# Encoder layer, MLP stage: the first two output tiles made together, the last square summed by TensorE, a function table loaded at another place

## What is computed

```python
hn = modulated_rms_norm(h, sh2, sc2)            # rms_norm(h) * (1 + sc2) + sh2, over 2048 features
u = dwconv_centred(hn @ w_up[l], w_ffn_conv[l]) + b_ffn_conv[l]   # 2048 -> 2 * 5632, 3 taps over tokens
u_gate, u_val = jnp.split(u, 2, axis=-1)
h = h + gt2[:, None, :] * ((jax.nn.silu(u_gate) * u_val) @ w_down[l])
return rms_norm(h) * final_norm
```

## Time and profile before

| | |
|---|---|
| median of 3 runs | 2656.44 us (2653.32 to 2656.96) |
| profiled execution, its own time | 2658.15 us |
| its span | 2656.5 us |
| TensorE matmul busy | 2560.8 us, 96% |
| DVE busy | 1425.2 us, 54% |
| ScalarE busy | 1022.2 us, 38% |
| mean granted clock of TensorE | 0.983 of full |

### The profile page before, as it was taken

The page is one execution under the profiler, slowest core; times in us unless marked ns, Lnnn a source line. Parts: engine busy times, 40 slices in busy tenths (PEclk is TensorE's granted clock), DMA queues, the critical chain, the costliest instruction groups (busy, mean ns, idle before and its releaser), DMA issues.

```text
span 2656.5 us, 35703 instructions
## 1 busy us (share of the span) xinstructions
PE 2560.8 (96%) x12302; PEld 2098.3 (79%) x12302; DVE 1425.2 (54%) x1854; ACT 1022.2 (38%) x1428; POOL 214.3 (8%) x286
## 2 busy tenths in 40 slices
PE   4999999999999899979999999999999999999997
PEld 4777788888887688857888888888888888888885
DVE  6736666666666655464444444444444444444454
ACT  4335435434434343334443234442344432222334
POOL 3401121121121112000000000000000000000000
PEclk7999999999999999999999999999999999999998
DMA  9933454454443535323333333333333323333333
GB/s 349 317 107 111 127 154 116 133 148 120 144 140 113 151 104 155 106 63 95 95 96 91 98 103 95 95 89 98 105 95 97 100 84 98 103 95 95 89 92 127
DMA packets 431664, 318.21 MB, mean 120 GB/s; under 512 B 12886, under 2 KB 403841, under 8 KB 431105
## 3 DMA queue, kind: packets, MB, share of 16 engines
q1 hardware_dynamic: 401648, 212.19, 27.8%
q0 software_dynamic: 29184, 104.87, 12.4%
q10 hardware_dynamic: 785, 0.51, 0.1%
HBM read 313.33 MB, written 4.19 MB: 120 GB/s over the span
## 4 chain that ended last, share of the span: by engine, by line
PE 92%; DVE 3%; DMA 1%; issue 1%; ACT 1%; POOL 0%; DVEq 0%; ACTq 0%; POOLq 0%
PE pw L1399 23%; PE pw L1401 23%; PE pw L1400 23%; PE pw L1383 2%; PE pw L1384 2%; PE pw L1385 2%; PE pd L1669 2%; PE pd L1692 2%; PE pd L1705 2%; PE pd L1652 1%; PE pd L1712 1%; DMA ka<-in_w_ada_dram 1%; DMA T<-in_w_ada_dram 1%; PE pd L1728 1%; PE pd L1723 1%
## 5 line engine op out<-in xcount | busy, mean ns | idle before, releaser
L1399 PE MATMUL pw<-act_hi,w_hi 128*128 128x512 f32 x2016 | 812.7, 403 | 13.9 <-DVE act_lo L1294 8.7
L929 DVE TENSOR_TENSOR w_lo<-raw,w_hi 128x1024 fp32r<-128x1024 f32 x426 | 520.7, 1222 | 519.2 <-ACT w_hi L555 516.7
L1401 PE MATMUL pw<-act_hi,w_lo 128*128 128x512 f32 x2016 | 787.3, 391 | 0.0
L1400 PE MATMUL pw<-act_lo,w_hi 128*128 128x512 f32 x2016 | 785.6, 390 | 0.0
L555 ACT ACTIVATE w_hi<-raw 128x1024 fp32r<-128x1024 f32 x426 | 450.1, 1057 | 503.3 <-PE pw L1401 408.6
L1399 PEld LDWEIGHTS pw<-act_hi,w_hi 128*128 128x128 f32 x2016 | 379.3, 188 | 106.6 <-issue 23.8
L1401 PEld LDWEIGHTS pw<-act_hi,w_lo 128*128 128x128 f32 x2016 | 378.9, 188 | 81.4
L1400 PEld LDWEIGHTS pw<-act_lo,w_hi 128*128 128x128 f32 x2016 | 379.7, 188 | 80.3 <-issue 6.9
L1399 PE MATMUL pw<-mh_hi,w_hi 128*128 128x512 f32 x704 | 276.0, 392 | 1.6 <-DVE w_lo L929 1.6
L1401 PE MATMUL pw<-mh_hi,w_lo 128*128 128x512 f32 x704 | 274.2, 389 | 0.0
L1400 PE MATMUL pw<-mh_lo,w_hi 128*128 128x512 f32 x704 | 274.0, 389 | 0.0
(11 more groups left out here) (278 smaller groups left out, 2639.2 us busy)
## 6 DMA issues: line engine op xcount, KB each, us to landing
raw<-in_w_up_dram SPq DMA_DIRECT2D x176, 512.0 KB, 4.0
ada_w<-in_w_ada_dram POOLq DMA_DIRECT2D x128, 512.0 KB, 4.4
raw<-in_w_in_dram SPq DMA_DIRECT2D x84, 512.0 KB, 3.9
raw<-in_w_down_dram SPq DMA_DIRECT2D x64, 384.0 KB, 3.4
raw<-in_w_down_dram SPq DMA_DIRECT2D x64, 320.0 KB, 3.1
raw<-in_w_out_dram SPq DMA_DIRECT2D x32, 512.0 KB, 4.4
DD<-in_w_ada_dram POOLq DMA_DIRECT2D x9, 512.0 KB, 8.1
EG<-in_w_ada_dram POOLq DMA_DIRECT2D x9, 512.0 KB, 7.0
```

Of the source, the lines that this page charges most:

```text
L929: V.tensor_tensor(w_lo[slot][:], raw[slot][:], w_hi[slot][:].bitcast(F32), ALU.subtract).then_inc(lo_made.sem, 1)
L1399: M(bank, w_hi[slot][:, k, :], hi[:, k0 + k, :], start=first, stop=False)
L1400: M(bank, w_hi[slot][:, k, :], lo[:, k0 + k, :], start=False, stop=False)
L1401: ins = M(bank, w_lo[slot][:, k, :], hi[:, k0 + k, :], start=False, stop=last)
```

## The change

Six parts.

- SP loads the first four units of the MLP otherwise: unit MLP0+i now holds feature tiles 4i to 4i+3 of both the first gate tile and the first value tile, side by side, in two transfers of 256 KB, the second counted on a semaphore of its own (up_in).
- TensorE's `first_up` does six matmuls for each normalised tile, three for either bank. The splits of units MLP0+2 and +3 stand on ScalarE behind act_hi of tiles 6 and 10, their low halves on DVE in the passes of tiles 8 and 12. Both banks end together.
- The first tile pair's copies, convolution, Silu and product are written out ahead of the loops, which start at pass 1 in chunk 0.
- The last square before the norm isn't added by DVE. TensorE sums sqacc (15 squares) and then sq into the same bank.
- ScalarE loads the table set of Ln and Exp by name at the start of the last chunk's down stage.
- In that stage DVE multiplies by the norm's weights before it adds the square, not after.

The bodies of `convolve` and `gated` are those of the loop before, moved out of it (L1315 to L1337), and left out here.

```diff
--- before.py
+++ after.py
...
-        q_in = sem("q_in")
+        q_in, up_in = sem("q_in"), [sem(f"up_in{i}") for i in range(2)]
...
-            with sp.Fori(0, CHUNKS) as c:
-                with sp.Fori(0, FC) as f:
+            def chunk(c, first=0):
+                with sp.Fori(first, FC) as f:
                     for part in range(2):
                         tile(MLP0 + MLP_PER * c + 4 * f + 2 * part, w_up, part * DFF + (c * FC + f) * P)
                 with sp.Fori(0, KT) as m:
                     u = MLP0 + MLP_PER * c + 4 * FC + 2 * m
                     for j, (k0, n_k) in enumerate(((0, 6), (6, FC - 6))):
                         load(j, u + j, w_down[bass.ds((c * FC + k0) * P, n_k * P), bass.ds(m * P, P)], n_k)
+
+            for i in range(4):
+                sp.wait_ge(lo_made.sem, MLP0 + i - 1)
+                by_tile = raw[i % 2][:].rearrange("p (k t) n -> p k t n", t=2)
+                for t, landed in enumerate((raw_in[i % 2], up_in[i % 2])):
+                    rows_i = w_up[4 * i * P:4 * (i + 1) * P, t * DFF:t * DFF + P]
+                    sp.dma_start(by_tile[:, :, t, :], rows_i.rearrange("(k p) n -> p k n", p=P)).then_inc(landed, 16)
+            chunk(0, first=1)
+            with sp.Fori(1, CHUNKS) as c:
+                chunk(c)
...
             split((OUT0 + KT) // 2, 1)
-            with act.Fori(0, KT // 2) as i:
+            with act.Fori(0, KT // 2 - 1) as i:
                 for j in range(2):
                     split((OUT0 + KT) // 2 + i + 1, j)
                     square(2 * i + j)
+            for j in range(2):
+                act.wait_ge(up_in[j], 16)
+                split(MLP0 // 2, j)
+                square(KT - 2 + j)
 
             def inverse_rms(i):
                 act.wait_ge(*ssum.after(i))
@@ -851,11 +865,27 @@
                 act.wait_ge(*h2_step.after(0, m + 1))
                 nc.scalar.activation(act_hi[:, m, :], hn2[:, m % 2, :], ACT.Identity, bias=mod[:, 48 + m:49 + m]) \
                     .then_inc(h2_hi.sem, 1)
-
-
-            def chunk(c, last=False):
+                if m in (6, 10):
+                    act.wait_ge(up_in[(6, 10).index(m)], 32)
+                    split(MLP0 // 2 + 1, (6, 10).index(m))
+
+            def first_up(part):
+                act.wait_ge(unit_used.sem, MLP0 + 4)
+                act.wait_ge(fconv_step.sem, 3 * part + 3)
+                nc.scalar.activation(gp[:, part, 1:S + 1], pw[part][:], ACT.Copy).then_inc(up_taken.sem, 1)
+
+            split(MLP0 // 2 + 2, 0)
+            first_up(0)
+            first_up(1)
+            split(MLP0 // 2 + 2, 1)
+            act.wait_ge(fconv_step.sem, 9)
+            nc.scalar.activation(cv[:, 0, :], cv[:, 0, :], ACT.Silu).then_inc(fsilu.sem, 1)
+            act.wait_ge(*fprod.after(0))
+            nc.scalar.activation(mh_hi[:, 0, :], prod[:], ACT.Copy).then_inc(mh_hi_made.sem, 1)
+
+            def chunk(c, first=0, last=False):
                 base = MLP0 // 2 + MLP_PER // 2 * c
-                with act.Fori(0, FC) as f:
+                with act.Fori(first, FC) as f:
                     n = FC * c + f
                     pair = base + 2 * f
 
@@ -881,12 +911,13 @@
                     if last:
 
                         act.wait_ge(out_taken.sem, KT * CHUNKS + m + 1)
-                        act.wait_ge(sqacc_step.sem, KT + 1 + m)
+                        act.wait_ge(sqacc_step.sem, KT + m)
                         nc.scalar.activation(sq[:], at(hTf, m), ACT.Square).then_inc(sq_made.sem, 1)
                         if j is not None:
                             turned(m - 2, j)
 
                 if last:
+                    nc.scalar.preload_act_table_set(LOG_EXP)
                     down(0)
                     down(1)
                     with act.Fori(1, KT // 2) as i:
@@ -902,7 +933,8 @@
                 nc.scalar.activation(otok[:, :, bass.ds(m * P, P)], pd[1 + j].rearrange("p (b n) -> p b n", n=P), ACT.Copy) \
...
-            with act.Fori(0, CHUNKS - 1) as c:
+            chunk(0, first=1)
+            with act.Fori(1, CHUNKS - 1) as c:
                 chunk(c)
             chunk(CHUNKS - 1, last=True)
...
-            with dve.Fori(0, KT // 2) as i:
+            def out_tile(i, j, last=False):
+                m = 2 * i + j
+                low((OUT0 + KT) // 2 + i + 1, j)
+                residual(OUT0 + KT + m + 1, m, pw[j][:], 32)
+                if not last:
+                    add_square(m)
+
+            with dve.Fori(0, KT // 2 - 1) as i:
                 for j in range(2):
-                    m = 2 * i + j
-                    low((OUT0 + KT) // 2 + i + 1, j)
-                    residual(OUT0 + KT + m + 1, m, pw[j][:], 32)
-                    add_square(m)
+                    out_tile(i, j)
+            out_tile(KT // 2 - 1, 0)
+            out_tile(KT // 2 - 1, 1, last=True)
...
                 if m:
                     h2_low(m - 1)
+                if m in (8, 12):
+                    low(MLP0 // 2 + 1, (8, 12).index(m))
             h2_low(KT - 1)
 
             V.memset(cv[:, 0, 0:1], 0.0).then_inc(fconv_step.sem, 3)
             V.memset(cv[:, 1, 0:1], 0.0).then_inc(fconv_step.sem, 3)
 
-            def chunk(c, last=False):
+            def convolve(n, part):
...
+
+            low(MLP0 // 2 + 2, 0)
+            convolve(0, 0)
+            low(MLP0 // 2 + 2, 1)
+            convolve(0, 1)
+            gated(0, 0)
+
+            def chunk(c, first=0, last=False):
                 base = MLP0 // 2 + MLP_PER // 2 * c
-                with dve.Fori(0, FC) as f:
+                with dve.Fori(first, FC) as f:
                     n = FC * c + f
                     pair = base + 2 * f
...
                     low(pair + 1, 0)
...
+                    gated(n, f)
 
                 def down(m, j, reused=True):
                     low(base + 2 * FC + m + 1, 0)
...
                     if last:
-                        dve.wait_ge(sq_made.sem, KT + m + 1)
-                        dve.wait_ge(sqacc_step.sem, KT + 1 + m)
-                        V.tensor_tensor(sqacc[:], sqacc[:], sq[:], ALU.add).then_inc(sqacc_step.sem, 1)
                         if reused:
                             dve.wait_ge(fin_sum.sem, m - 1)
                         dve.wait_ge(out_taken.sem, KT * CHUNKS + m + 1)
                         V.tensor_scalar(hn2[:, j, :], at(hTf, m), col[:, bass.ds(V_FN + m, 1)], None, ALU.mult) \
                             .then_inc(fin_made.sem, 1)
+                        dve.wait_ge(sq_made.sem, KT + m + 1)
+                        dve.wait_ge(sqacc_step.sem, KT + m)
+                        V.tensor_tensor(sqacc[:], sqacc[:], sq[:], ALU.add).then_inc(sqacc_step.sem, 1)
 
...
-            with dve.Fori(0, CHUNKS - 1) as c:
+            chunk(0, first=1)
+            with dve.Fori(1, CHUNKS - 1) as c:
                 chunk(c)
 
...
-            pe.wait_ge(sqacc_step.sem, KT + 1)
+            pe.wait_ge(sqacc_step.sem, KT)
             pe.wait_ge(*x2_taken.after(0))
-            M(pd[0], ones, sqacc[:], start=True, stop=True).then_inc(ssum.sem, 1)
+            M(pd[0], ones, sqacc[:], start=True, stop=False)
+            pe.wait_ge(sq_made.sem, KT)
+            M(pd[0], ones, sq[:], start=False, stop=True).then_inc(ssum.sem, 1)
+
+            def first_up():
+
+                pe.wait_ge(out_taken.sem, KT)
+                pe.wait_ge(up_taken.sem, 2)
+                for i in range(4):
+                    pe.wait_ge(lo_made.sem, MLP0 + i + 1)
+                    for k in range(4):
+                        m = 4 * i + k
+                        pe.wait_ge(*h2_lo.after(0, m + 1))
+                        for t in range(2):
+                            w = 2 * k + t
+                            M(pw[t][:], w_hi[i % 2][:, w, :], act_hi[:, m, :], start=m == 0, stop=False)
+                            M(pw[t][:], w_hi[i % 2][:, w, :], act_lo[:, m, :], start=False, stop=False)
+                            ins = M(pw[t][:], w_lo[i % 2][:, w, :], act_hi[:, m, :], start=False, stop=m == KT - 1)
+                    ins.then_inc(unit_used.sem, 1)
 
...
-                def up(f, ready=None):
+                def up(f):
                     for j in range(2):
                         pe.wait_ge(out_taken.sem, KT * (c + 1) - 1 + j)
                         pe.wait_ge(up_taken.sem, 2 * (FC * c + f) + j + 1)
-                        whole(base + 2 * f + j, pw[j][:], ready=ready if j == 0 else None)
...
-                    up(0, ready=lambda k: h2_lo.after(0, k + 1))
+                    first_up()
                 with pe.Fori(1 if first else 0, FC) as f:
                     up(f)
                 if last:
...
-            pe.wait_ge(sqacc_step.sem, 2 * KT + 1)
+            pe.wait_ge(sqacc_step.sem, 2 * KT)
             for b in range(NB):
                 ins = M(pd[0][:, b:b + 1], sqacc[:, b * P:(b + 1) * P], ones[:, 0:1], start=True, stop=True)
             ins.then_inc(ssum.sem, 1)
```

(13 more changed lines are left out.)

27 lines of the change are left out of this document (9 added, 18 removed).

## The result

The changed kernel takes 2642.75 us (median of 5 runs, 2642.39 to 2644.31), the kernel before 2656.44 beside it: ratio 0.995, 95% interval 0.994 to 0.9961, 13.7 us less. The profiled execution took 2643.47 us, its span is 2641.8.

The account below looks back on a forecast made before the run. TensorE, with 92% of the chain, was taken to bound the kernel. Projection-to-MLP seam 9.3 plus end 2.4 minus early load 1.45 gave 10.25 us, taking the median 2656.44 to 2646.2; range 2641.5 to 2651.

Parts of the forecast that it names:

- Bound and rigid part: MLP after its first two output tiles: TensorE waited 1.2 us in 1290, so an earlier start ends it equally earlier.
- Last square, 1.3: Between output projection and MLP: last square summed by TensorE shortens the chain by 1.3 us, bounds 0.75 and 1.4.
- Split waits 0.8: Normalisation stretch: ScalarE's split waits until unit MLP0 is used, delaying later tiles 0.4 to 1.1 us, taken as 0.8.
- Two low halves on DVE, 2.3: Normalisation stretch: low halves of units MLP0+2 and +3 between the tiles add 2.3 us on DVE.
- The copy's pause, 0.85: Before the third output tile: both banks are full at once, so TensorE idles 0.85 us behind ScalarE's copy.
- Early load, 1.45: Last chunk's down stage: the table load ahead of the split delays split and TensorE, loss 1.45 us, bounds 0 and 1.5.
- End, 2.4: End of the kernel: new order (0.7) and two table loads gone (1.7) gain 2.4 us, between 1.7 and 3.0.
- (b): Rival: the table loads at the end stay and the early one is paid; gain 8.5 us, 2647.9; chance 0.09.
- (c): Rival: the early load finds cover, or no table load is on the path; gain 11.7 us, 2644.7; chance 0.06.
- (e): Rival: the split loads of the first MLP units land late, path 29 us longer at worst, 2675; chance 0.04.
- (a): Rival: in the normalisation stretch the clock rises 3 to 7 us later; gain about 8, 2648; chance 0.09.
- (d): Rival: half clock through the whole normalisation stretch, 2661.3; chance 0.06, shared with any other loss of half the gain.

Follow-up runs that it names:

- tiles alone: The first two output tiles made together, without the three other parts, against the kernel before: 2647.78 us against 2655.79 (0.997).
- sum in one: The changed kernel with the matmul on sqacc moved behind the wait for the last square: 2646.41 us against 2656.42 for the kernel before (0.9959).

## Why the prediction was right, point by point

It said 2646.2 with 10.25 us of gain; the stages of the change gave 11.8, the medians 13.7 and 11.4. The places and the mechanism are as forecast; two of its terms were off the same way, 0.7 at the split and 0.6 at the end. Of the 3.5 us between the forecast and the median, the remaining 2 or so are luck with where the seam starts.

- *Bound and rigid part.* Right: 1302.69 and 1302.82 us, although 66 table loads vanished from it. TensorE's waits from 1205 to 2500 come to 1.6 us.
- *Last square, 1.3.* Measured 1.33 in the changed kernel. The step hid a condition, though: its gain was taken as moving "Everything from Ln on". With the old tile order, all of it is lost to a second half-clock stretch, in both profiles of the kernel with the square alone. The prediction looked for the clock's cost only where the clock was already low.
- *Split waits 0.8.* Too much: 0.14, and 0.2 when the changed kernel ran again. The step that failed is "from 1172.8 some 15 at 0.43 until the clock rises at 1179.2". It moved the first matmul earlier and left the rise of the clock where it stood, 6.4 us behind it. In the trace of before the rise came 5.2 us after the first matmul, in the changed kernel 3.2, and unit MLP0's last matmul had started (1176.65) before ScalarE came to the split at 1177.16. Where the rise did come late, with the tiles alone and with the sum in one, the split waited 1.05 and 0.97 us and the stretch was 0.7 and 0.6 longer: the price was right, its condition didn't hold. Twice the matmuls are not the reason: those two kernels have them, and the square-only kernels rose after 3.4 us without them. What goes with the early rise is a first matmul soon after the fall, which is the last square's doing.
- *Two low halves on DVE, 2.3.* Measured 2.0 (after against before, and again when they were taken away). With the split this puts the last low half 23.06 us after the first matmul instead of 24.1; 1.0 is all that the seam gave more than forecast (10.36 against 9.3).
- *The copy's pause, 0.85.* Measured 0.94, and 0.95 when it was taken away.
- *Loads free.* Right, with room: four times as many were free too.
- *Early load, 1.45.* Measured 1.46. The gap behind mh_hi is 0.02, the load 1.28, the split 0.01 behind it. The Trainium skill ("ScalarE: Activation LUTs", What ACT_TABLE_LOAD costs) counts some 1.38 of drain besides; by that, as an estimate, the loss would be about 2.8. No switch in these traces shows it, so the measurement decides.
- *End, 2.4.* Order 0.71 and loads 1.68, as forecast. The 0.6 beyond them is the granted clock, which in after fell only with the last transposes. The sum had the transposes and the squares at half clock, as in the earlier trace rows.
- *Rivals.* (b), (c) and (e) are out: no load at the end, the early one paid in full, the transfers early. (a) and (d) are out too: in none of the profiles did the clock rise later after the first matmul than in before, and in most it rose sooner.
- *Not foreseen.* Of the medians' 13.7, about 2 are the spread of where the seam starts. The seam's stages repeat to 0.1 (the stretch 26.04, 26.00 and 26.05), but the end of the changed kernel lies between 4.34 and 5.31 with the clock; the medians of a few runs gave the gain as 13.7 and 11.4.

Open: whether the square alone brings the second fall or only met it (the clock in before doesn't fall in the same pause of 2.02 us, and TensorE is about as busy ahead of it); and what sets the start of the memset.

## What to carry to other kernels

When two consumers of slowly made tiles can be served at once, give the engine both, and count what the maker has to do in between: here 11 us of matmuls went into a stretch where TensorE was waiting anyway, at the price of 2.0 on DVE and a pause of 0.9 for a bank. Put a table load behind the last activation that anyone waits for, not ahead of the next one: the same load cost 1.46 us in one place and nothing two splits later. And don't add parts by their chains: a step that shortens a chain by 1.24 us lost it again, in both profiles taken, where the clock fell in the thin work behind it.

## What the hardware showed beyond that

- The granted clock fell for 3.4 us in a wait of 2.02 us in two profiles, with TensorE 65% busy before it in the one shown (13.28 of 20.50), and didn't in a third with the same wait (before, 71%) nor when unused matmuls filled both. It cost 1.5 us.
- It rose 3.0 to 3.5 us after the MLP's first matmul in ten profiles, where that matmul came 3.3 to 3.8 us after the fall, and 5.0 to 5.2 in three (before, tiles only, sum in one), where it came 5.0 us or more after it. Three or six matmuls per tile stand in either group, so how dense the work was didn't decide. The Trainium skill ("TensorE: Matmul & The Clock Gate", What's actually happening) has activity release the half clock; these agree as far as the rise always came after TensorE had work again.
- The same work reached the last projection residual up to 4.3 us apart in different executions, 1.6 of it from one stretch of half clock right behind a wait of 1.9 us, which 5 of 14 profiles have (0.51 against 1.00 above, at the same DMA share of 0.88).
- Transfers of 512, 256 and 64 KB landed 4.0, 3.3 and 2.0 us after their issue: an eighth of the bytes took half the time.
- A table load stood at the head and at the Silu of each of 33 passes of the loop, and at neither in the changed kernel, where a Silu stands ahead of the loop: 66 loads went with an edit that doesn't name them. That the Silu's place is the reason was forecast, not tested apart.
